# Seven block products for eight in a feed-forward layer's first matrix product, with GpSimd and VectorE sharing the added work

## What is computed

```python
for l in range(DEPTH):                      # 2 layers; prompt and sample rows alike
    xn = rmsnorm(xp, norm_mix[l])
    q, k, v, qi, ki, wi, u, gv = project(xn, w_in[l], pos_p)
    a = dsa_prompt(q, qi, wi, k, v, ki, pos_p)
    gvn = rmsnorm(gelu(gv), gate_norm[l])
    bmix = gelu(u) * spatial_prompt(gvn, w_spatial[l], b_spatial[l])      # the gating
    xp = xp + concatenate([a, bmix], -1) @ w_out[l]
    h = relu(rmsnorm(xp, norm_ffn[l]) @ w_ff1[l])                         # first product
    xp = xp + (h * h) @ w_ff2[l]                                          # second product
```

## Time and profile before

| | us |
|---|---|
| median of three runs | 1340.86 (1340.78 to 1342.54) |
| the profiled execution, its own time | 1341.55 |
| its span | 1339.8 |
| TensorE busy in the span | 1296.0 (97%) |
| VectorE busy | 707.0 (53%) |
| ScalarE busy | 498.3 (37%) |
| GpSimd busy | 224.2 (17%) |

### The profile page before, as it was taken

One profiled execution on the slowest core, in us unless ns is written; L12 is line 12 of the kernel. 1 busy time (PEld: TensorE's weight loads), 2 busy tenths in 40 slices (PEclk: granted clock), 3 DMA queues, 4 the chain that ended last, 5 costly groups with the idle time before them and its releaser, 6 DMA issues.

```text
span 1339.8 us, 23532 instructions
## 1 busy us (share of the span) xinstructions
PE 1296.0 (97%) x9903; PEld 1247.6 (93%) x9903; DVE 707.0 (53%) x1318; ACT 498.3 (37%) x904; POOL 224.2 (17%) x249
## 2 busy tenths in 40 slices
PE   6999998999999999999999999999999999999997
PEld 6888778999999999999988987799999999999997
DVE  5598853554444444444648987255444444444453
ACT  5467742332133132133346666243312312312322
POOL 1265434200000000000214755320000000000011
PEclk8999999999999999999999999899999999999998
DMA  6212112322232223222331121132222232232221
GB/s 183 68 33 64 33 33 81 101 79 79 85 89 80 79 79 95 79 80 79 84 91 49 48 64 32 33 107 85 86 79 79 87 88 79 79 89 85 80 64 71
DMA packets 177962, 102.46 MB, mean 76 GB/s; under 512 B 7432, under 2 KB 176320, under 8 KB 177856
## 3 DMA queue, kind: packets, MB, share of 16 engines
q1 hardware_dynamic: 177856, 100.95, 25.9%
HBM read 96.98 MB, written 3.95 MB: 75 GB/s over the span
## 4 chain that ended last, share of the span: by engine, by line
PE 85%; DVE 6%; POOL 4%; issue 2%; ACT 1%; DMA 1%; SPq 0%; DVEq 0%; POOLq 0%; ACTq 0%
PE bank L1685 69%; PE bank L1428 8%; PE bank L1585 2%; DVE late L1130 1%; PE bank L1562 1%; POOL late L632 1%; PE bank L1545 1%; PE bank L1424 1%; POOL ring_lo L648 1%; POOL late L670 1%; DVE late L1099 1%; DVE gsq L1162 1%; DMA late<-in_x_prompt 1%; PE bank L1496 1%; PE bank L1605 1%
## 5 line engine op out<-in xcount | busy, mean ns | idle before, releaser
L715 ACT ACTIVATE ring_hi<-ring_raw 128x1024 fp32r<-128x1024 f32 x176 | 185.2, 1053 | 279.8 <-PE bank L1685 248.5
L1685 PE MATMUL bank<-vh,ring_hi 128*128 128x288 f32 x1280 | 275.9, 297 | 3.0 <-POOL ring_lo L648 3.0
L1685 PE MATMUL bank<-vl,ring_hi 128*128 128x288 f32 x1280 | 275.3, 297 | 0.0
L1685 PE MATMUL bank<-vh,ring_lo 128*128 128x288 f32 x1280 | 275.3, 297 | 0.0
L966 DVE TENSOR_TENSOR ring_lo<-ring_raw,ring_hi 128x1024 fp32r<-128x1024 f32 x150 | 192.5, 1284 | 64.0 <-ACT ring_hi L715 56.8
L1685 PE MATMUL bank<-xh,ring_hi 128*128 128x288 f32 x1024 | 219.7, 296 | 1.9 <-issue 1.9
L1685 PE MATMUL bank<-xh,ring_lo 128*128 128x288 f32 x1024 | 219.3, 296 | 0.0
L1685 PE MATMUL bank<-xl,ring_hi 128*128 128x288 f32 x1024 | 219.3, 296 | 0.0
L1685 PEld LDWEIGHTS bank<-vh,ring_hi 128*128 128x128 f32 x1280 | 207.6, 190 | 3.7 <-DVE vl L1226 2.0
L1685 PEld LDWEIGHTS bank<-vh,ring_lo 128*128 128x128 f32 x1280 | 207.5, 190 | 0.0
L1685 PEld LDWEIGHTS bank<-vl,ring_hi 128*128 128x128 f32 x1280 | 207.5, 190 | 0.0
(11 more groups left out here) (196 smaller groups left out, 1606.6 us busy)
## 6 DMA issues: line engine op xcount, KB each, us to landing
ring_raw<-in_w_ff SPq DMA_DIRECT2D x128, 512.0 KB, 3.9
ring_raw<-in_w_in SPq DMA_DIRECT2D x32, 512.0 KB, 3.8
ring_raw<-in_w_out SPq DMA_DIRECT2D x32, 128.0 KB, 2.8
ring_raw<-in_w_out SPq DMA_DIRECT2D x16, 256.0 KB, 3.2
late<-in_x_prompt SPq DMA_DIRECT2D x4, 512.0 KB, 5.6
out_y_prompt<-late SPq DMA_DIRECT2D x4, 512.0 KB, 3.4
w_sp<-in_w_spatial SPq DMA_DIRECT2D x2, 512.0 KB, 4.3
gate_bc<-in_gate_norm SPq DMA_DIRECT2D x2, 256.0 KB, 4.8
```

Source lines behind the costliest of these rows:

```text
L715: s.activation(ring_hi[:, n % NSLOT, :], ring_raw[:, n % NRAW, :], ACT.Copy).then_inc(hi_ready, 1)
L1685: last = mm(bank[unit_bank(u) + half][:, 0:HALF], w[:, k, :], a[:, k, HALVES[half]], start=k == 0 and w is wh and a is ah, stop=k == KT - ...
```

## The change

The first product goes pair by pair: two units, that is 256 hidden features, are one 2x2 block product with contraction blocks too. Feature tiles alternate between the two blocks of the contraction (even tiles, odd tiles), the two units are the two blocks of the output features, the two column halves the two blocks of rows. Winograd's variant of Strassen's form makes the eight block products with seven. In the order in which they run they are called R1, R6, R2, R7, R5, R4, R3; each has a contraction of 512 (four slabs), three matmuls a slab, one bank: 12 matmuls. Four of the seven weight operands are sums or differences of blocks of the weights, made anew for each pair; of the activations' operands three are differences, made once a layer (`xth`, `xtl`), and one replaces a block in `xh`, `xl`.

- GpSimd makes the four weight sums of a pair (`weight_sums`), and two of the seven remainders of 128x512 (`half_lo_pool`, for R5 and R3). VectorE makes the other five (`half_lo_dve`), ScalarE all seven high parts (`half_hi`). A ring place holds two such halves; halves are made five products ahead (`AHEAD`).
- ScalarE copies the bank of R1 (`p1`); VectorE reads the banks of the other six, R5's twice, seven adds of 128x288 (`read`), and takes relu and square in one operation (`squared`) and the remainder (`hidden_low`). Products take the eight banks in turn.
- Raw weights of the feed-forward part have four places instead of two; the new ones are `pl_a`, idle there.
- GpSimd gates three of five row tiles, VectorE the other two. GpSimd makes slab 17's remainder before the gating, VectorE slab 18's.
- Cache outputs are issued on SP's queue before the output product's weights, no longer after; two query transposes move up by two steps and the last top-k may start four steps earlier; the reciprocal for `r2b` moves behind the first stage of the first product.

```diff
+    NPR, PAIRS, FU = 7, KT // 2, FT // 2
+    GU = KT // 2
+    R1, R6, R2, R7, R5, R4, R3 = range(NPR)
+    POOL_LO = [R5, R3]
+    DVE_LO = [i for i in range(NPR) if i not in POOL_LO]
+    AHEAD = 5
...
-    SCORED = dict(zip(INDEX_TILES, [19, 23, 27, 44]))
+    SCORED = dict(zip(INDEX_TILES, [19, 23, 27, 40]))
...
-    QT_AT = {41: 0, 42: 1, 45: 2, 46: 3, 47: 4}
+    QT_AT = {41: 0, 42: 1, 43: 2, 44: 3, 45: 4}
...
-        POOL_SPLITS = range(6, S_OUT + NSLOT)
+        POOL_SPLITS = range(6, S_OUT + NSLOT - 1)
...
+        def turn_bank(g, n):
+            return 7 - n % 8 if g == 0 else n % 8
...
+        def half_source(h):
+            u, i = divmod(h, NPR)
+            a, b = (raw_at[RAW_OF["ff", 2 * u + e][0]].rearrange("p (k e n) -> p k e n", e=2, n=P) for e in range(2))
+            return {R1: a[:, :, 0, :], R2: a[:, :, 1, :], R4: b[:, :, 1, :], R5: b[:, :, 0, :],
+                    R7: w_sums[0], R6: w_sums[1], R3: w_sums[2]}[i]
...
+                def weight_sums(u, ks):
+                    a, b = (raw_at[RAW_OF["ff", 2 * u + e][0]].rearrange("p (k e n) -> p k e n", e=2, n=P) for e in range(2))
+                    s3, s2, s4 = w_sums
+                    a11, a12, a21, a22 = a[:, :, 0, :], a[:, :, 1, :], b[:, :, 0, :], b[:, :, 1, :]
+                    for k in ks:
+                        out, x0, x1, op = [(s3, a11, a21, ALU.subtract), (a21, a21, a22, ALU.add), (s2, a21, a11, ALU.subtract),
+                                           (s4, a12, s2, ALU.subtract)][k]
+                        if k == 0:
+                            for e in range(2):
+                                place_, count_ = RAW_OF["ff", 2 * u + e]
+                                pool.wait_ge(w_ready[place_], count_)
+                        if k >= 1:
+                            pool.wait_ge(w_sum, 4 * u + k)
+                        if u and k != 1:
+                            pool.wait_ge(*half_lo(NPR * (u - 1) + (R7, None, R6, R3)[k]))
+                        g.tensor_tensor(out, x0, x1, op).then_inc(w_sum, 1)
...
-                    if s == U_GELU_AT + 2:
-                        for t in TURN:
-                            gated(t)
-                sum_squares(KT * 2 * l)
+                for t in TURN[::2]:
+                    gated(t)
+                sum_squares(KT * 2 * l, range(KT // 2))
+                for u in range(FU * l, FU * (l + 1)):
+                    if u % GU == 0:
+                        weight_sums(u, range(4))
+                    if u == FU * l:
+                        sum_squares(KT * 2 * l, range(KT // 2, KT - 2))
+                    if R5 in POOL_LO:
+                        half_lo_pool(u, R5)
+                    if u % GU < GU - 1:
+                        weight_sums(u + 1, range(3))
+                    if R3 in POOL_LO:
+                        half_lo_pool(u, R3)
+                    if u == FU * l:
+                        sum_squares(KT * 2 * l, range(KT - 2, KT))
+                    if u % GU < GU - 1:
+                        weight_sums(u + 1, range(3, 4))
...
+                    for h in range(base, end + 2):
+                        u, i = divmod(h, NPR)
+                        if i == R6 and h < end:
+                            act.wait_ge(f_done, h)
+                            if u:
+                                act.wait_ge(f_read, READS * (u - 1) + READ_OF[R2])
+                            s.activation(p1, bank[product_bank(h - 1)][:, 0:HALF], ACT.Copy).then_inc(p1_copied, 1)
+                        if h > base + 1 and i < 2:
+                            m = 1 - i
+                            act.wait_ge(h_made, 2 * u - m)
+                            s.activation(vh[:, (2 * (u - 1) + m) % KT, :], h32[:, m, :], ACT.Copy).then_inc(vh_ready, 1)
+                        if h < end and base + NPR - 1 <= h + AHEAD < end:
+                            half_hi(h + AHEAD)
...
+            def first_rows(l, j):
...
+                if e == 0:
+                    v.tensor_tensor(xg[:, 0, HALVES[1]], b12, xg[:, 0, HALVES[0]], ALU.subtract).then_inc(t1_made, 1)
+                    dve.wait_ge(xp_hi, 3 * n + 1)
+                    v.tensor_tensor(xl[:, j, :], xg[:, 0, :], xh[:, j, 0:TOK].bitcast(F32), ALU.subtract).then_inc(xp_ready, 1)
+                    return
...
+                link(v.tensor_tensor(tt[:, 0, :], b22, xg[:, 0, HALVES[1]], ALU.subtract))
+                v.tensor_tensor(tt[:, 1, :], b22, b12, ALU.subtract)
+                v.tensor_tensor(tt[:, 2, :], b21, tt[:, 0, :], ALU.subtract).then_inc(tt_made, 1)
...
+                v.tensor_tensor(xtl[:, :, p, :], tt, xth[:, :, p, :].bitcast(F32), ALU.subtract).then_inc(xp_ready, 1)
...
+                def read(out, h, other):
+                    v.tensor_tensor(out, bank[product_bank(h)][:, 0:HALF], other, ALU.add).then_inc(f_read, 1)
...
+                def product(fu, i, ps):
...
+                    for p in ps:
+                        if i in (R6, R7, R4):
+                            m = (R6, R7, R4).index(i)
+                            ah, al, part = xth[:, m, p, :], xtl[:, m, p, :], 2
+                        else:
+                            part, half = {R1: (0, 0), R5: (0, 1), R2: (1, 0), R3: (1, 1)}[i]
+                            ah, al = (a[:, 2 * p + part, HALVES[half]] for a in (xh, xl))
+                        if fu == 0:
+                            pe.wait_ge(xp_ready, 3 * (PAIRS * l + p) + part + 1)
+                        for w, a in ((wh, ah), (wh, al), (wl, ah)):
+                            last = mm(bank[b][:, 0:HALF], w[:, p, :], a, ...)
...
+                        product(fu, R1, pairs).then_inc(f_done, 1)
+                        if fu == 0:
+                            product(fu, R6, pairs[:-1])
+                            product(fu, R2, pairs)
+                            product(fu, R6, pairs[-1:]).then_inc(f_done, 2)
...
+                    for j in range(KT):
+                        unit(KT * (g + 1) + j, [k ^ 1 for k in range(KT)])
```

510 lines of the change are left out of this document (364 added, 146 removed).

## The result

The changed kernel took 1327.57 us (median of four, 1326.79 to 1328.70) beside 1341.70 for the kernel before on the same chip: a ratio of 0.9895, 95% interval 0.9878 to 0.9912, that is 1.05% faster. The forecast was 1309 and 2.4%: the right sign, a time inside the range (1285 to 1338), and less than half of the gain. The profiled execution took 1326.79 us with a span of 1324.9, 14.8 less than before where the sum had 32.7.

What follows compares the result with a forecast made beforehand. TensorE, busy 97% of the span, was taken as the bound. 1341.55 - 51.2 (matmuls) + 22.4 (stage waits) + 4.4 (first stages) - 1.9 (old wait) - 6.4 (attention's end) = 1308.9 us, say 1309; range 1285 to 1338.

Steps and rivals of the forecast that it cites:

- Matmuls: First product: 384 fewer matmuls at 0.1333 us each, 51.2 us less; nothing charged for twelve in a row into one bank.
- The pace of a full pair: First product: VectorE and GpSimd take turns, so a full pair takes 14.0 us against TensorE's 11.2, 2.8 late.
- The lateness after the first pair: Start of a stage: taking turns with GpSimd, VectorE ends its step of the seventh product about 3.5 us late.
- What TensorE feels of it: First product's stages: lateness of 9.1 us against 6.3 of look-ahead costs 2.8 a stage, +22.4 us for eight.
- The sentence on the variant without GpSimd's remainders: First product: R5's and R3's remainders on GpSimd add 1.2 us of turns to a pair; not part of the sum.
- The first stage of a layer: First product's start: activations need sums and remainders of three more blocks, and R5 comes late; 2.2 us a layer, +4.4.
- First product's start and end of attention: Old 0.96 us wait at the first product goes, -1.9; slab and gating changes save 3.2 a layer, -6.4.
- Edits at nothing: Moved reciprocal, cache outputs ahead on SP's queue and extra raw places' queue waits are covered and cost nothing.
- B: Rival: nothing comes back at a change of hand; full pairs 15.2 us, 1328 us; chance 0.19 with neighbourhood to 1338.
- C: Rival: ScalarE, VectorE and GpSimd queues wait in a ring; serial pairs of 17.4 us, 1363 us; chance 0.15 with D.
- A: Rival: look-ahead hides it all; full pairs of 12.2 to 13 us, no stage loss, 1286.5 us; chance 0.18.
- D: Rival: product form gains nothing because a matmul's price lies elsewhere, in weight loading; 2%.

Runs made afterwards that it cites:

- hidden_late: Changed kernel with VectorE's two hidden remainders of a pair made behind the next pair's remainders for R1 and R6, no longer ahead of them; 1320.18 us.
- r3_only: Changed kernel with R5's remainder moved from GpSimd to VectorE; GpSimd keeps the weight sums and R3's remainder; 1292.13 us.
- squares_late: As hidden_late, with relu, square and the square's high part on ScalarE, where VectorE made the square and ScalarE one copy; 1341.81 us.
- early_sums: Changed kernel with a layer's first-pair weights loaded early into pl_a and, in its first stage, the second pair's first three sums ahead of R5's remainder; 1319.21 us.
- r3_early_ss: Changed kernel with R5's remainder on VectorE, a layer's first-pair weights loaded early into pl_a, and the sums-of-squares read three steps earlier; 1282.68 us.

## Why the prediction was right or wrong

**Matmuls: right.** 9519 of them, 0.1326 us in a stage without waits; -53.3 for -51.2. The stretch read as a first product is a second product. The row that follows it is a first product but for 0.95 us at its start. It has the same length, so the price stands, but ScalarE is busier in it, 17.5 us for 9.8:

```profile
362.30:413.50 51.20, 51.20 (x386) 51.20 (x385) 21.89 (x25) 17.52 (x29) 0.00 (x0) 1.00 0.28 80
```

**The pace of a full pair: right, by two errors that cancel.** 14.09 us for 14.0. Its own work was put at 9.7 us (rows added up; 8.5 by starts) and the stalls at 4.3 (5.6).

**The lateness after the first pair: right in size, in part by luck.** 3.5 us were forecast at the seventh product; TensorE finished it at 372.78 and VectorE read it at 376.29. But 1.48 of the 3.5 is VectorE's wait behind GpSimd's third sum, for which the working had no term; it put all of it down to turns.

**What TensorE feels of it: the step that failed first.** I held the lateness at a pair's last product against the look-ahead of 6.3 us. But VectorE's work isn't spread evenly over a pair: behind that read come a square, a remainder and both hidden remainders, 7.03 us in which TensorE runs two products (3.2), and only then the remainder for the next pair's R1. There VectorE was 3.5 + 3.85 = 7.4 late, 1.1 over the look-ahead, and at this place TensorE waits:

```profile
385.17 0.40 PE L2058 MATMUL bank<-xh,ring_hi 128*128 128x288 f32 x1 [1.10 <-DVE ring_lo L1214]
```

The next full pair adds 14.09 - 11.14 = 2.95, so 4.0 in all; 4.27 were lost and 2.8 forecast. hidden_late, which moves the two hidden remainders behind, brought the stage to 47.24, 2.7 above the 44.54.

**The order that I took as given.** The working lists "R5, three sums, R3 and the fourth sum" as GpSimd's work in the stage, and prices it at 1.28 us each, 7.7 a pair; beside VectorE they took 1.56 on the mean, and GpSimd was busy 31.2 us in a stage where 20 to 25 were forecast. It also didn't ask why the sums were in the stage at all, while GpSimd had nothing to do for 19 us ahead of it. The answer was in the order's row, a remainder with a wait for ScalarE's high part, and in the ring places, which the last slabs of the second product hold. r3_only, which takes this one remainder out of the queue, is worth 35 us, twice what the forecast was short of. The sentence on the variant without GpSimd's remainders (1.2 us of turns a pair) had the sign and missed the mechanism. The Trainium skill, Perfetto Trace Analysis, section "Optimizing Scalar/DVE Operations", warns that work moved from VectorE to GpSimd might not help, since they share a port. R3's remainder agrees with that: moved, it gave neither gain nor loss (1292.13 beside 1292.99). R5's lost 22 us (1314.93), and that came from its place in the queue. The section also says that moving work from a full VectorE to ScalarE may make sense; squares_late did that and lost 21.6 us.

**The first stage of a layer: the step that failed most.** Forecast 5.0 us a stage (2.8 and 2.2), measured 12.4 and 11.2. I priced the way of the last unit's activations and R5's own delay, and neither what queues behind R5 (three sums, then R6's high part and remainder of the next pair) nor when the first weights land (240.6, from a place that the output product's slabs hold until then). I wrote that the two new places leave queue waits "a pair's time"; the two old ones come first in the loading order, and the new ones would have been free. early_sums won 4 us of it by these two edits, and r3_early_ss 8.1 and 6.9. The larger part hangs on the sums' length: with narrow sums and every wait kept, 2.1 us of the loss were left. Whether VectorE's stalls or the sums' own lateness weigh more in this stage, no run separates. The half clock, which the prediction named as what would make it wrong, was a part: 6.8 us of it in layer 0's first stage, 10.2 in layer 1's. The prediction has such a stretch cost as much again as it lasts; the later stages show 1.5 us of cost for a stretch of 3.40.

**First product's start and end of attention: right, and better by the clock.** The waits that went are 3.1 and 0.96 us a layer for 3.2 and 0.96 forecast. What is left of the 6.0 and 6.5 us is 1.9 and 2.5; I put it down to the low level that stood behind the old wait and stayed away. The prediction had up to 3 for both and took none.

**Edits at nothing: right.** The second product's 51.19 us show no trace of the reciprocal; TensorE waits for no transfer behind the inputs, so the outputs moved on SP's queue show no cost either.

**Rivals.** B came nearest by its time, 1328, but not by its cause: it had pairs of 15.2 us. C's chain of waits was there once a stage, in the first pair (VectorE idle for 1.48 us), but not in a full pair, where VectorE is never idle. A was wrong for this kernel. r3_only has A's outcome, later stages that wait for nothing, though not its cause: a full pair takes VectorE 13.2 us there (bank reads at 371.69 and 384.88), over A's 12.2 to 13. D was not there: a matmul kept its price.

## What to carry to other kernels

Look-ahead is a matter of the worst step in a cycle, not of the mean: follow the late engine's queue to the one operation for which the fast engine waits, and count what stands ahead of it. In a queue that runs in order, an operation that waits for a buffer holds all that stands behind it; ask of each idle stretch what would have fitted there, before asking which engine should do the work. An engine that has room can still make a busy one later, if what moves to it stands ahead of what the busy one waits for; squares_late looks like such a case, though no run isolated it.

## What the runs showed of the hardware that I had not expected

One more GpSimd addition of 128x512, 1.29 us alone, takes 0.93 to 1.0 us from a VectorE that is busy all the time, over four, six and eight operations a pair alike (pairs of 13.38, 14.09 and 17.33 us); GpSimd's own operation grows to 1.56 on the mean. A granted clock of 0.5 came after an idle time of 1.75 us in three of six stages with the same idle times to a hundredth; no row here tells which. In kernels whose stages don't wait it never came in a later stage.
